# Moving the second pair of weight parts by 16 bytes, and the branch rows to other places modulo 256

## The reference, cut to what matters

```
# first block, layer l (x is 256 x 1024)
h      = x @ w_in            # q, k, v of three attentions, gates
o      = [nsa(h), mla(h), fox(h)]            # "branch rows"
x      = LN(a*x + (sum_b gate_b * (o_b @ w_br_b)) @ w_mix_out)
x      = LN(a*x + cross_attention(x, mem))
x      = LN(a*x + gelu(x @ w_up) @ w_down)   # 1024 -> 4096 -> 1024
# second block, layer l
h      = rms_norm(x) * (1 + scale) + shift
o      = [pool(h), retention(h), rwkv7(h)]
x      = x + gate * ((sum_b gate_b * (o_b @ w_branch_b)) @ w_out)
```

## Time and profile before

| what | value |
|---|---|
| median of the runs | 1628.04 us |
| the profiled execution | 1630.29 us, its span 1628.5 us |
| PE matmul busy | 1571.9 us (97%), 16984 matmuls |
| PE weight loads | 1438.3 us (88%) |
| DVE / ACT / POOL | 1008.2 (62%) / 714.3 (44%) / 560.5 (34%) |
| granted TensorE clock, mean | 0.987 |

### The profile page before, as it was taken

The page is one execution under the profiler, slowest core; times in us unless marked ns, Lnnn a source line. Parts: engine busy times, 40 slices in busy tenths (PEclk is TensorE's granted clock), DMA queues, the critical chain, the costliest instruction groups (busy, mean ns, idle before and its releaser), DMA issues.

```text
span 1628.5 us, 37963 instructions
## 1 busy us (share of the span) xinstructions
PE 1571.9 (97%) x16984; PEld 1438.3 (88%) x16984; DVE 1008.2 (62%) x1657; ACT 714.3 (44%) x1126; POOL 560.5 (34%) x452
## 2 busy tenths in 40 slices
PE   9999999999999999999999999999999999999988
PEld 8898988899888989988999899989988899998886
DVE  4365486877773555676777877764336769644257
ACT  4544434554454444454444455423322555332323
POOL 3654613000309636312000303716552009255530
PEclk9999999999999999999999999999999999999999
DMA  9422365686545322465775444533233445333332
GB/s 361 163 105 104 122 228 202 255 305 255 190 161 213 136 99 104 158 243 233 288 293 204 184 171 146 189 130 112 100 132 129 157 156 193 131 132 127 109 107 91
DMA packets 43956, 281.68 MB, mean 173 GB/s; under 512 B 5145, under 2 KB 5273, under 8 KB 14353
## 3 DMA queue, kind: packets, MB, share of 16 engines
q1 hardware_dynamic: 42192, 270.13, 45.3%
q0 software_dynamic: 1600, 9.12, 1.5%
HBM read 278.17 MB, written 1.06 MB: 171 GB/s over the span
## 4 chain that ended last, share of the span: by engine, by line
PE 79%; DVE 12%; issue 4%; ACT 3%; POOL 2%; DMA 0%; POOLq 0%; SPq 0%; ACTq 0%; DVEq 0%
PE ps L573 77%; PE ps L581 3%; DVE part0l L1407 2%; DVE part1l L1407 2%; DVE rows L1831 1%; DVE Pr L1828 1%; ACT part0h L2460 1%; ACT Xh L2460 0%; DVE Xl L1422 0%; DVE small L1438 0%; DMA ring<-in_w 0%; DVE raw L1953 0%; DVE mgx L2085 0%; DVE x L1431 0%; DVE gates L2174 0%
## 5 line engine op out<-in xcount | busy, mean ns | idle before, releaser
L2460 ACT ACTIVATE part0h<-ring 128x1024 fp32r<-128x1024 f32 (+1 forms) x216 | 213.0, 1035 | 236.7 <-PE ps L573 222.8
L2460 ACT ACTIVATE part1h<-ring 128x1024 fp32r<-128x1024 f32 (+1 forms) x216 | 215.8, 1047 | 228.0 <-PE ps L573 215.7
L573 PE MATMUL ps<-Xh,part1h 128*128 128x256 f32 x968 | 276.2, 285 | 7.1 <-DVE Xl L1422 2.4
L573 PE MATMUL ps<-Xh,part0h 128*128 128x256 f32 (+1 forms) x952 | 275.4, 289 | 2.2 <-DVE Xl L1422 1.3
L573 PE MATMUL ps<-Xl,part1h 128*128 128x256 f32 x968 | 269.2, 278 | 0.7 <-issue 0.7
L573 PE MATMUL ps<-Xh,part1l 128*128 128x256 f32 x968 | 269.1, 278 | 0.0
L573 PE MATMUL ps<-Xl,part0h 128*128 128x256 f32 (+1 forms) x952 | 268.4, 282 | 0.3 <-issue 0.3
L573 PE MATMUL ps<-Xh,part0l 128*128 128x256 f32 (+1 forms) x952 | 268.4, 282 | 0.0
L2956 POOL TENSOR_TENSOR part0l<-ring,part0h 128x512 fp32r<-128x512 f32 x144 | 184.2, 1311 | 141.0 <-ACT part0h L2460 140.9
L2956 POOL TENSOR_TENSOR part1l<-ring,part1h 128x512 fp32r<-128x512 f32 x144 | 183.3, 1306 | 119.2 <-ACT part1h L2460 119.2
L1407 DVE TENSOR_TENSOR part1l<-ring,part1h 128x1024 fp32r<-128x1024 f32 (+1 forms) x144 | 181.4, 1299 | 50.2 <-ACT part1h L2460 50.0
(11 more groups left out here) (439 smaller groups left out, 3335.1 us busy)
## 6 DMA issues: line engine op xcount, KB each, us to landing
ring<-in_w SPq DMA_DIRECT2D x211, 1024.0 KB, 4.8
hid<-in_ada SPq DMA_DIRECT2D x36, 512.0 KB, 5.9
hid<-in_w SPq DMA_DIRECT2D x6, 1024.0 KB, 10.9
rows<-in_lnrow POOLq DMA_DIRECT2D x6, 1024.0 KB, 9.6
fqk<-in_ada SPq DMA_DIRECT2D x6, 512.0 KB, 7.1
cq<-in_ada SPq DMA_DIRECT2D x6, 512.0 KB, 6.9
gates<-in_c SPq DMA_DIRECT2D x2, 1536.0 KB, 8.3
ring<-in_w SPq DMA_DIRECT2D x4, 512.0 KB, 5.4
```

The costliest lines, as they stand in the source:

```text
L573: return e.matmul(o, a, b, start=st, stop=sp)
L2460: return e.activation(o, a, ACT.Copy)
```

## The change

`pair` takes a `lead` (columns skipped at the front of each tensor of the pair) and a `spare` (columns added to its size). The parts are now made by `pair`: pair 0 as before, pair 1 with a lead of 4 columns (16 bytes) and 64 spare columns in each of its two tensors. What comes after moves by 512 bytes. The first block's `A` gets a lead of 12 columns and 64 spare. `vcbd` gives up its own tile and shares `raw1`, which frees the room. The filler below the second block's A rows grows by 56 columns (layer 0) and 48 (layer 1).

Start modulo 256 after: part0 128, part1 144; X, P, R 64; A 112; A0 32; A1 0.

```diff
-        def pair(stack, name, **dims):
+        def pair(stack, name, lead=0, spare=0, **dims):
             n = int(np.prod(list(dims.values())))
-            return [v(stack.enter_context(nc.sbuf_tensor(name + h, [128, n], F32R))[:, :], **dims) for h in "hl"]
+            return [v(stack.enter_context(nc.sbuf_tensor(name + h, [128, n + spare], F32R))[:, lead:lead + n], **dims)
+                    for h in "hl"]
...
-        self.parts = [[ctx.enter_context(nc.sbuf_tensor(f"part{i}{h}", [128, PW], F32R))[:, :] for h in "hl"]
-                      for i in range(SPLIT)]
+        self.parts = [pair(ctx, f"part{i}", lead=4 * i, spare=64 * i, c=PW) for i in range(SPLIT)]
...
-        self.A1 = pair(s1, "A", k=8, n=256)
+        self.A1 = pair(s1, "A", lead=12, spare=64, k=8, n=256)
...
-        self.vcbd = v(S("vcbd", 512), g=2, c=256)
+        self.vcbd = v(self.raws[1], g=2, c=256)
...
-                sb(sa, f"below A{l}", 7168)
+                sb(sa, f"below A{l}", 7168 + (56, 48)[l])
```

## The result

| kernel | median | lowest to highest | profiled run (span, mean granted clock) |
|---|---|---|---|
| before | 1627.74 us, 12 runs | 1624.36 to 1634.25 | 1630.29 us (1628.5, 0.987) |
| after | 1638.46 us, 12 runs | 1632.50 to 1643.37 | 1636.31 us (1634.5, 0.993) |

The ratio is 1.0065, with a 95% interval of 1.0052 to 1.0078: 10.7 us slower. The forecast was 1619 with a range of 1608 to 1637; the measured time lies just above it, at rival 2.

A forecast was written before the change was run, and what follows sets the result against it. The prediction took the spacing of matmul starts on TensorE as the bound. Its terms, −2.1 − 5.2 − 1.2 − 0.4 = −8.9 us off the median 1628.0, gave 1619 us, with a range of 1608 to 1637.

The forecast's parts named there:

- rival 2: MLP and attention projections: shifted pair turns wide-spaced where it was close; +5 to +14 us, middle 1637; chance 0.19.
- What bounds the kernel: Whole kernel: TensorE busy 97% of the span, so the end is set by how far apart matmuls start.
- Part 1, 256 columns: Matmuls on part 1, moved 16 bytes: 40% of a possible 5.4 us gain, −2.1 us; at worst 10.3 us lost.
- the wide mode: 256-column matmuls about 0.1178 us apart instead of 0.1133, 4.5 ns each; address may help decide it, but not alone.
- `dn`, 512 columns: 816 `dn` matmuls, A moved 48 bytes: half the excess spacing goes, −5.2 us; bounds −10.4 and +3.7.
- The supposed floor, 0.2156: Best spacing in us assumed for 512-column fp32r matmuls, from plain float32 ones of 256 columns; 0.0127 us under `dn`'s 0.2283.
- rival 3: More gain than forecast: `dn` goes to its floor, −17 us in all, 1611 us; chance 0.12.
- Part 1 with X stationary, 512 columns: 192 matmuls: half the excess spacing goes, −1.2 us; bounds −2.4 and +0.9.
- A2: Second block's A moved to 32 and 0: layer 1's 96 wide-spaced matmuls become close, −0.4 us.
- `br` and `xo`: First block's products that also read A: counted as unchanged, within ±1 us.
- The writers: ACT, DVE and POOL writing part 1 at a start 16 bytes further on: 0 us.
- `vcbd`: Sharing `raw1` adds no wait, and PE waits on nothing new: cost 0.

The follow-up runs named there:

- raw1_only: Only `vcbd` sharing `raw1`, all starts modulo 256 as before, against the kernel before: 1627.46 us, ratio 1.0003.
- a_only: Only A moved to 112 and A2 to 32 and 0, `vcbd` in `raw1`, against the kernel before: 1629.80 us, ratio 1.0017.
- p16: Only the second pair of parts moved by 16 bytes to 144, `vcbd` in `raw1`, against the kernel before: 1639.02 us, ratio 1.0058.

## Why the prediction was wrong

**What bounds the kernel** was right. The whole result lies in the spacing of matmuls; no engine, queue or wait took a part, and the chain over the MLP has the same shape.

**Part 1, 256 columns: the step that failed.** The prediction took 40% of the possible gain here, −2.1 us. Measured: (118.7 − 114.5) x 2672 = +11.2 us with X moving, and (119.3 − 117.4) x 540 = +1.0 with the part moving, above its upper bound of +10.3. The working held the wide mode to be entered mostly by chance, because one product had both spacings at the same bytes. That observation was sound, and the close shares at −64 show it again, 46 to 76% in all layouts with X at 64 or 96. The inference was not: at distance −64 both spacings occur at the same starts, but without that distance the close mode hardly occurs. That a stretch takes its mode from how matmul and weight load fell together when it began, as the prediction put it, is shown by no run. A mode that holds for 70% of the matmuls can only get a little more common and can become very much rarer. The prediction said as much of the MLP under rival 2, "any change of mode there is a loss", and gave it 0.19.

**`dn`, 512 columns: the largest term, mis-signed.** −5.2 us was taken. Measured: part 1 (232.5 − 228.8) x 368 = +1.4, part 0 (228.3 − 228.8) x 368 = −0.2. That addresses alone can change it was right; that half of the excess would go was a choice between bounds with no row under it. The lowest ever seen, 226.9, is 1.9 ns under the 228.8, where the prediction had allowed up to 12.7 and taken 6.3. The supposed floor, 0.2156 from plain float32, was another kind of matmul's, as rival 3 said against itself.

**Smaller terms.** Part 1 with X stationary, 512 columns: −1.2 taken, (231.2 − 229.1) x 169 = +0.4 measured. A2: −0.4 taken; at 118.6 to 120.1 ns for 115.5 to 116.1 it is about (+3.1 and +4) x 92, +0.6. `br` and `xo`, "unchanged, within ±1": 117.2 with part 0, 119.9 with part 1 for 113.4, +1.9 over 362 intervals. P's and R's products with part 1, which the prediction's count left out: 118.7 for 114.0, +0.8. The writers at 0 were right (1221 ns for 1220), and `vcbd` too (raw1_only).

**The sum.** With part 0 (+0.3 x 2564, +0.8) these terms make about +18 us, and the medians differ by 10.7. Over the first 10200 matmuls the account closes: the full-clock intervals add 10.9 us (256 columns, activation moving), 0.6 (part moving) and 1.4 (512 columns), waits and long intervals take back 1.0, and the kernel after is 11.9 us late. In the last 6800, mostly the second block, the lateness falls to 6.0. There 83 of the 171 intervals of double length became full-clock ones, 83 x 0.096 = 8 us saved; without them spacing adds 5 us, and some 3 us come back in waits and other work. The double ones vary between profiles of every layout (68 to 171, 132 in raw1_only, which is laid out as before); had the kernel before had 132, it would have been 39 x 0.096 = 3.7 us shorter and the difference 9.7, near the medians'. What sets their number was not tested. The 3 us are mostly shorter waits: PE's idle time behind the first 10200 matmuls is 23.1 us before and 20.4 after.

The Trainium skill, "TensorE: Matmul & The Clock Gate", Part 2, step ①, says that the next weights' load takes no read bandwidth from the running matmul. Carried over to start addresses, as the prediction did, it would put every row of the experiments' table at 1.000. For fp32r the runs disagree, from 0.9977 to 1.0182 with nothing but starts moved. They don't show that it is the load that takes something from the matmul. The Trainium skill, "TensorE: Matmul & The Clock Gate", "Back-to-back issue gap", gives N/2.4 + 2.5 ns for the gap of isolated matmuls at the upper clock level, an estimate of 109 and 216 ns for 256 and 512 columns, and about 131 ns for 512 columns in a stream of loads and matmuls. The fp32r forms here agree with neither: none had a mean under 113.3 and 226.9.

## What to carry to other kernels

Where PE is the bound and matmuls are fp32r, as here, the starts of both operands modulo 256 are a tuning parameter, worth 2% from best to worst in this kernel; measure the start-to-start spacing of each product's form, and keep the distance of a layout that is close-spaced. When one operand moves, even by 4 bytes or to make room for something else, move its partners by the same amount, and try a common shift last. A mode that is seen both ways at the same bytes doesn't show that the bytes are irrelevant: ask first whether it is seen at all at another distance.

## What the runs showed that was not expected

- A difference of 4 bytes between two operands' starts, in tensors of 2048 columns, changes the spacing of 512-column matmuls from 228.8 to 239.5 ns and takes the 256-column close share from 70% to none.
- The sign matters: the same two tensors give 0.1179 us with one as the stationary operand and 0.1133 with the other.
- The close share at distance −64 varies between executions of like layouts (a_only's profile, its highest run but one at 1635.09 us, had 46 to 49%, and p16's part 0 had 50%; before 70 to 74%). Shifted by 16 or 48 bytes together it was 88 to 90% in all three kernels.
- Why −64, what PE waits for at the other distances, and whether the running matmul's own weights or the next one's count, is not known.
